# A fused transformer and expert layer on one core: the gather of the second expert pair by products with a 0/1 matrix instead of an indirect transfer

## The reference

```python
def expert_choice_ffn(h, w_router, w_gate, w_up, w_down):
    B, T, D = h.shape
    cap = EC_CAPACITY_FACTOR * T // N_EXPERTS          # 64
    aff = jax.nn.softmax(einsum('btd,de->bte', h, w_router), axis=-1)
    g, idx = lax.top_k(aff.transpose(0, 2, 1), cap)
    xs = jax.vmap(lambda hb, ib: hb[ib])(h, idx)       # the gather
    a = einsum('becd,edf->becf', xs, w_gate)
    u = einsum('becd,edf->becf', xs, w_up)
    y = einsum('becf,efd->becd', silu(a) * u, w_down) * g[..., None]
    return zeros((T, D)).at[idx].add(y)                # the spread

x  = x + mod[2] * merge_heads(o_mla, o_na, ...)        # called x1 in the kernel
h2 = modulate(rms_norm(x, g_norm2), mod[3], mod[4])
x  = x + mod[5] * expert_choice_ffn(h2, ...)
```

## Time and profile before

| | |
|---|---|
| time, median of 3 runs | 1972.55 us (1971.76 to 1973.77) |
| the profiled execution's own time | 1973.06 us |
| its span, first to last instruction | 1971.2 us |
| TensorE busy | 1893.7 us, 96% |
| VectorE, ScalarE, GpSimd busy | 909.6, 461.6 and 201.9 us |
| read from and written to HBM | 584.85 and 16.79 MB |

### The profile page before, as it was taken

The page is one execution under the profiler, slowest core; times in us unless marked ns, Lnnn a source line. Parts: engine busy times, 40 slices in busy tenths (PEclk is TensorE's granted clock), DMA queues, the critical chain, the costliest instruction groups (busy, mean ns, idle before and its releaser), DMA issues.

```text
span 1971.2 us, 26157 instructions
## 1 busy us (share of the span) xinstructions
PE 1893.7 (96%) x10242; PEld 1220.9 (62%) x10242; DVE 909.6 (46%) x1875; ACT 461.6 (23%) x1224; POOL 201.9 (10%) x434
## 2 busy tenths in 40 slices
PE   4999999999999999999999999999989899998999
PEld 2579888888889999888875334435344353534433
DVE  5568887773266776645755231303113031221343
ACT  4233323122256766631142100000000000000000
POOL 0003112011134543100000000000000000000000
PEclk9999999999999999999999999999999999999999
DMA  9967988883122112352549999999999999999999
GB/s 403 420 230 288 345 312 283 292 305 107 62 68 81 58 47 71 141 214 86 212 166 395 420 429 431 432 428 433 430 432 431 430 432 430 431 430 431 414 427 368
DMA packets 70451, 603.34 MB, mean 306 GB/s; under 512 B 6829, under 2 KB 24493, under 8 KB 35257
## 3 DMA queue, kind: packets, MB, share of 16 engines
q1 hardware_dynamic: 56736, 590.06, 73.9%
q10 hardware_dynamic: 13160, 10.03, 1.5%
q0 software_dynamic: 432, 1.57, 0.2%
HBM read 584.85 MB, written 16.79 MB: 305 GB/s over the span
## 4 chain that ended last, share of the span: by engine, by line
PE 53%; DMA 8%; DVE 1%; ACT 0%; issue 0%; DVEq 0%; ACTq 0%
PE SM L1416 9%; PE TM L1416 9%; DMA arena<-in_w_twos 7%; PE TM L1468 6%; PE SM L1468 6%; PE TR L1363 2%; PE MJ L1363 2%; PE SN L1403 1%; PE TM L1152 1%; PE TM L1180 1%; PE TM L1182 1%; PE SM L1182 1%; PE SM L1180 1%; PE TM L1181 1%; PE SM L1181 1%; DMA wor<-in_w_out 1%
## 5 line engine op out<-in xcount | busy, mean ns | idle before, releaser
L1416 PE MATMUL SM<-arena 128*64 128x512 f32 x1024 | 251.5, 612 | 27.6 <-DMA arena<-in_w_twos 27.6
L1416 PE MATMUL TM<-arena 128*64 128x512 f32 x1024 | 243.8, 595 | 0.0
L2093 DVE SCALAR_TENSOR_TENSOR arena<-arena,csil 128x512 f32<-128x512 f32 x240 | 180.4, 752 | 13.2 <-DMA arena<-in_w_mod 3.2
L1416 PEld LDWEIGHTS SM<-arena 128*64 128x64 f32 x1024 | 71.9, 138 | 163.1 <-issue 161.6
L1416 PEld LDWEIGHTS TM<-arena 128*64 128x64 f32 x1024 | 77.6, 139 | 147.2 <-issue 147.2
L1468 PE MATMUL TM<-arena,cst 128*64 128x512 f32 x512 | 116.9, 598 | 0.0
L1468 PE MATMUL SM<-arena,cst 128*64 128x512 f32 x512 | 114.9, 597 | 0.0
L2002 DVE TENSOR_TENSOR wl<-wr,wh 128x1024 fp32r<-128x1024 f32 (+3 forms) x59 | 74.5, 1265 | 70.3 <-ACT wh L1538 70.3
L1538 ACT ACTIVATE wh<-wr 128x1024 fp32r<-128x1024 f32 (+3 forms) x59 | 62.4, 1083 | 188.8 <-PE TN L928 140.4
L2425 DVE TENSOR_TENSOR brow<-cst,rope_t 128x512 f32<-128x512 f32 x7 | 4.8, 692 | 219.6 <-PE MJ L1389 219.6
L1793 ACT CAST y_hi<-arena 128x512 fp32r<-128x512 f32 x31 | 19.2, 618 | 368.1 <-DVE arena L2473 341.8
(11 more groups left out here) (456 smaller groups left out, 3703.5 us busy)
## 6 DMA issues: line engine op xcount, KB each, us to landing
arena<-in_w_twos SPq DMA_DIRECT2D x68, 4096.0 KB, 23.2
arena<-in_w_mod SPq DMA_DIRECT2D x96, 1024.0 KB, 6.4
arena<-in_w_first SPq DMA_DIRECT2D x41, 2048.0 KB, 11.9
arena<-in_w_last SPq DMA_DIRECT2D x15, 2048.0 KB, 23.7
wr<-in_w_na SPq DMA_DIRECT2D x24, 1024.0 KB, 6.8
wor<-in_w_out SPq DMA_DIRECT2D x16, 1024.0 KB, 5.2
xT<-in_tokens_t SPq DMA_DIRECT2D x4, 1536.0 KB, 12.8
arena<-in_w_qkv SPq DMA_DIRECT2D x8, 640.0 KB, 5.2
```

The lines of the kernel that those rows point to most:

```text
L1416: mm = pe.matmul(GU[b][64 * e:64 * e + CAP, :], xsT[:, k, 64 * e:64 * e + CAP], w[:, 2 * (b // 2) + e, (b % 2) * NB:(b % 2 + 1) * NB], sta ...
L2093: ve.scalar_tensor_tensor(acc, row, c, acc, ALU.mult, ALU.add).then_inc(mod_step, 1)
```

## The change

It takes out everything that served the indirect fetch for pair 1: `rows_1`, `member_1`, `members_ahead`, `find_rows(1)`, `take_index(1)`, ScalarE's scaling of `rows_1`, and GpSimd's two indirect transfers. Pair 1 goes through the same products as pairs 2 to 7. Since only `x1_d[1]` is now read, blocks 0 and 1 of `x1` are not stored, and the waits count the four stores of block 2 alone. Pair 0 keeps its indirect fetch. The diff, with the removal of definitions left out:

```diff
@@ sync
-            store_x1(0, 2 * OUT_BLOCKS - 1)
             sp.wait_ge(y_full, end_of(3 * MODB - 3, LT - 1) + 1)
             moe_load(1)
-            store_x1(1, 2 * OUT_BLOCKS - 1)
             sp.wait_ge(y_full, end_of(3 * MODB - 2, LT - 1) + 1)
             store_x1(2, 2 * OUT_BLOCKS - 1)
             moe_load(4)
@@ tensor
             def gather(pair, q):

                 if q == 0:
-                    if pair == 2:
+                    if pair == 1:
                         pe.wait_ge(x1_scaled, LT * MODB)
-                    pe.wait_ge(member_set, pair + 2)
+                    pe.wait_ge(member_set, pair + 1)
                     pe.wait_ge(pay_set, 2 * pair)
                 if q == 1:
                     pe.wait_ge(mt_set, pair)
                 pe.wait_ge(xt2_free, 16 * pair + max(4 * (q - 1), 0))
                 dst = (TR, MJ)[q % 2]
-                if pair == 1:
-                    if q == 0:
-                        pe.wait_ge(rows_set, 2)
-                    for i in range(4):
-                        k = 4 * q + i
-                        mm = pe.transpose(dst[:, i * P:(i + 1) * P], rows_1[:, k * P:(k + 1) * P], ident[:])
-                    mm.then_inc(xt2_full, 1)
-                    return
                 for i in range(4):
                     k = 4 * q + i
                     for tile in range(LT):
...
             def turn_act(pair, more):

                 if pair == 0:
-                    pe.wait_ge(idx_set, 3)
+                    pe.wait_ge(idx_set, 2)
...
-                    if pair == 0 and k == 7:
-                        find_rows(1)
@@ scalar
-            sc.wait_ge(x1_out, 16 * LT * (MODB - 1))
             sc.wait_ge(e_rsd, 2 * LT)
             for nb in range(MODB):
+                if nb == MODB // 2:
+                    sc.wait_ge(x1_out, 16 * LT)
                 if nb == MODB - 1:
                     sc.wait_ge(rows_out, 16 + 16 * LT)
...
-                if pair == 0:
-                    sc.wait_ge(rows_1_in, 32)
-                    sc.activation(rows_1, rows_1, ACT.Copy, scale=rows_rs[1]).then_inc(rows_set, 1)
@@ gpsimd
-            po.wait_ge(x1_out, 16 * LT * (MODB - 1))
+            po.wait_ge(x1_out, 16 * LT)
             po.wait_ge(rows_out, 16 + 16 * LT)
             po.indirect_dma_start(rows_0, None, x1_d[1], bass.IndirectOffsetOnAxis(ap=rows_idx[0], axis=0)).then_inc(rows_0_in, 16)
-            po.wait_ge(idx_set, 3)
-            for i in range(2):
-                po.indirect_dma_start(rows_1[:, i * HALF:(i + 1) * HALF], None, x1_d[i],
-                                      bass.IndirectOffsetOnAxis(ap=rows_idx[1], axis=0)).then_inc(rows_1_in, 16)
@@ vector
             take_slots()
-            members_ahead()
             take_first(9)
-            take_index(1)
```

More of the change, by code:

```diff
@@ L484, in build_layer @@
         y_hi = [own(f"y_hi{i}", (156 + 2 * i) * K, NB) for i in range(2)]
-        member_1 = arena.take(152 * K, LT, P)
         rows_0 = arena.take(148 * K, HALF)
-        rows_1 = arena.take(152 * K, D)
         picked = arena.take(156 * K, SEQ)[0:N_EXP]
@@ L633, in build_layer @@
             sem(n) for n in ("silu_done", "act_done", "at2_full", "at2_free", "y_done"))
-        idx_full, idx_set, x1_out, rows_0_in, rows_1_in, rows_set = (
-            sem(n) for n in ("idx_full", "idx_set", "x1_out", "rows_0_in", "rows_1_in", "rows_set"))
+        idx_full, idx_set, x1_out, rows_0_in, rows_set = (
+            sem(n) for n in ("idx_full", "idx_set", "x1_out", "rows_0_in", "rows_set"))
         y_high, y_low, mt_full, mt_set, add_full, acc_done = (
@@ L1365, in gather, with find_rows @@
                 mm.then_inc(xt2_full, 1)
[L1367 to L1371, removed]
+            def find_rows():
+                pe.wait_ge(idx_set, 1)
                 for tile in range(LT):
-                    mm = pe.matmul(SN[:, 0:2], (member, member_1)[pair][:, tile, :], token_no[:, tile, :], start=(tile == 0), stop=(tile == LT - 1))
+                    mm = pe.matmul(SN[:, 0:2], member[:, tile, :], token_no[:, tile, :], start=(tile == 0), stop=(tile == LT - 1))
                 mm.then_inc(idx_full, 1)
@@ L1379, in rows_of @@
                 if pair == 1:
-                    pe.wait_ge(member_set, 3)
+                    pe.wait_ge(member_set, 2)
                 for tile in range(LT):
@@ L1482, in _ @@
                     if pair == 0 and k == 0:
-                        find_rows(0)
+                        find_rows()
                     if pair == 0 and k == 5:
@@ L2433, in add_scales @@
                 ve.tensor_copy(token_no[:, :, 1], e_rs).then_inc(idx_set, 1)
[L2435 to L2440, removed]
             def take_index(pair):
```

## The result

| | before | changed |
|---|---|---|
| median | 1972.48 us (4 runs, 1971.76 to 1973.77) | 1983.85 us (4 runs, 1982.48 to 1985.65) |
| ratio | | 1.0059, 95% interval 1.0045 to 1.0072 |
| profiled execution, its span | 1973.06, 1971.2 us | 1982.48, 1980.7 us |
| TensorE busy | 1893.7 us | 1905.2 us |
| read, written | 584.85, 16.79 MB | 583.80, 14.69 MB |

The change costs 11.4 us where 8.0 were forecast. The profiled execution is the quickest of the four of the changed kernel.

What follows compares the result with a forecast made beforehand. The weight stream was taken to bound the kernel, TensorE counting through freed slots: 11.8 us added less 3.8 us of cushion gives 8.0; 1973.06 + 8.0 = 1981.1, less 0.5 for the median, 1980.5 us; range 1976.5 to 1984.5.

Steps and rivals of the forecast that it cites:

- What bounds the kernel: Expert stage: DMA engines full with weights at 421 to 429 GB/s; TensorE matters before 1310 us by freeing slots for loads.
- The rival that nothing notices: Loads for down-piece slots: queue fed far enough ahead, added work hides in 27.6 us of TensorE waits; 1969.6 us, 5%.
- Stores left out, zero: Eight 256 KB stores on SyncE around piece 1: leaving them out is worth zero, bound 0.4 us.
- The indirect transfers, 2.9 us of stream, hidden: GpSimd's 1.05 MB for pair 1: weight stream up to 2.9 us ahead at 1110 us, counted as worth nothing.
- TensorE's addition, 11.8 us: Pair 1's four groups: products 14.9 us in place of transposes 2.3, less 0.8 us of lost row-number products; no new wait.
- The slip, 11.8 - 3.8 = 8.0 us: Loads at 1130 to 1165 us: slots freed 11.8 us later, queue covers 3.8, so the weight stream ends 8.0 us later.
- The hole: Sign in the profile: DMA share well under 1 for about 8 us between 1143 and 1155 us, the queue run empty.
- the cushion of 3.8 us: Earlier work queued at issue, 1130 to 1165 us: shortest landing 11.3 less 7.5 on an empty queue; later slots cost only beyond it.
- The start of a piece on an empty queue, 2.6 us: Start and completion cost, read from 1024 KB output-projection loads: 5.0 us to landing, 2.4 us of it data.
- The later cushion of 5.9 us: Queue for later double pieces, 18.3 us to landing: covers TensorE's relative lag of 3.8 us, so nothing more is lost.
- The third rival: Pair 1's longer groups bring new TensorE waits, or the queue empties more than once: all 11.8 us arrive, 1984.4 us, 10%.
- The forecast's own case: Stream slips by 8.0 us to 1980.5 us; with start-cost uncertainty and run spread 1977 to 1982.5 us; 78%.

Runs made afterwards that it cites:

- the late groups: Changed kernel, gather groups 1 to 3 moved into the pair's own gate and up pieces: all pairs 1975.74 against 1972.38 us; pairs 1 to 3 alone 1973.13 against 1972.76.
- the groups of pairs 1 to 3 late: Changed kernel, gather groups 1 to 3 moved behind own gate and up pieces 2, 6, 10 for pairs 1 to 3 alone: 1973.13 against 1972.76 us, ratio 1.0004.
- A delay of 2.6 us: Kernel before with 23 more transposes of the same block ahead of pair 1's group 2, nothing else changed: 1974.32 against 1972.29 us, ratio 1.0011.
- the second median of the changed kernel: Changed kernel run again, unchanged, on the same chip as the products-alone version: 1984.77 us (1981.75 to 1987.17), ratio 1.0068.

## Why the prediction was nearly right

- **What bounds the kernel.** Right. The stream of weights sets the end, and TensorE's progress counts only through the slots. Shown by the late groups: same work, 11 us less time. The rival that nothing notices fell, and with it at this place the Trainium skill's measure of TensorE's headroom, weight-load busy share (Perfetto Trace Analysis, Identifying the Most-Contended Engine): at 41% of it, 11.4 us of added TensorE work cost 11.4 us. With the groups of pairs 1 to 3 late the same work did hide, in a longer queue and in TensorE's later waits, which no busy share tells apart.
- **Stores left out, zero.** Right, +0.5 us with an interval over zero when done alone.
- **The indirect transfers, 2.9 us of stream, hidden.** Hidden, yes: with and without them 1984.6 and 1984.8 us. The size was too large: 1.7 us of stream by 1130 us, and by the medians 0.5 us of time where no products follow.
- **TensorE's addition, 11.8 us.** 11.4 in the trace, with no new wait.
- **The slip, 11.8 - 3.8 = 8.0 us.** This is the step that failed, in size: 8.0 us were forecast and 11.4 and 12.4 measured. The hole is there, with its 8 us. But the step took the cushion of 3.8 us as free to use and the stream as whole again right behind the late load. A delay of 2.6 us, inside the cushion, already cost 2.0, and the second load behind the hole landed 3.3 us late. In the changed kernel's profile 2.3 us are lost ahead of the hole and 2.4 behind it. The losses make up for nearly the whole cushion: where pair 1 is 2.0 to 11.4 us late with the clock at its upper level, the cost by the medians lies within 1.0 us of that.
- **The start of a piece on an empty queue, 2.6 us.** The piece behind the hole landed 7.9 us after its issue, 3.0 over its data. The 2.0 us that the prediction sets beside it stand in a section of the Trainium skill (DMA: Bandwidth & Descriptors, Anatomy of one DMA) on transfers that GpSimd issues; these loads are SyncE's.
- **The later cushion of 5.9 us.** Right: TensorE made up the rest at its waits, 27.6 to 24.0 us, and from 1160 us on the stream is at 429 GB/s.
- **The third rival, +11.8 us because nothing is cushioned.** Its sum is the better one, but by another mechanism than the one it named: no new wait of TensorE appeared, and the queue ran empty once. The rest came from the DMA side, from the thin queue on both sides of the hole.

With the cushion struck out, the forecast would have been 1984.4 us.

That the time fell into the stated range is in part luck. The forecast's own case, with its 78%, ended at 1982.5 us, below both medians measured. The range reached further only to take in the third rival, and the second median of the changed kernel, 1984.77 us, lies just outside even of that.

## What to carry to other kernels

Where a stream of loads sets the time, look at each stretch for how long a load takes from issue to landing: that is how far work can be added to the engine that frees the buffers. Do not spend the last of it, since a queue down to its last load already moves less. Move added work to where that time is long; here the same products cost 11 us among the down pieces, where loads had 11 to 15 us to landing, and 0.4 us (at most 2.6 by the interval) among the gate and up pieces of pair 1, where they had 12 to 21 in the kernel before, and of the two pairs behind it.

## What the runs showed of the hardware that was not expected

A DMA queue that holds one 2 MB load or none loses more than the gap. Behind a hole the second load landed 3.3 and 2.1 us beyond the 4.9 us spacing in the two profiles of the changed kernel, and with the queue just not empty the rate fell to 348 GB/s at a DMA share of 0.97. The cause of this loss is open; no run here separates the single engines' shares of a load.

One stretch of the program, with TensorE's wait of 1.2 to 1.3 us in front of it, met a granted clock of 0.50 for about 3 us in four profiled executions and of 1.00 in ten. It costs 1.6 us on one group of products, and a reader of a single profile could take it for an effect of the change.
